# Three changes to the order of work in a one-layer decoder block: the loading of x, the spreading of a block inverse, the place of a router product

## The chip, the core and the metric

The kernel runs on one NeuronCore of a Trainium2 chip. Five engines work side by side, each through its own list of instructions in order: TensorE (PE, matmuls, with a separate column for its weight loads, PEld), VectorE (DVE), ScalarE (ACT), GpSimd (POOL) and SyncE (SP, which here only issues DMAs). ACT and SP both issue DMA transfers; an engine that waits on a semaphore holds up everything behind the wait in its own list. The metric is the device time of one execution in microseconds (us).

## The reference

One layer with 1024 tokens of width 1024, all in fp32. Cut to what matters:

```python
mod = silu(c) @ w_ada + b_ada            # six vectors: shift, scale, gate, twice (adaLN)
h = rmsnorm(x, g1) * (1 + sc1) + sh1
x1 = x + gt1 * hybrid_mixer(h)           # 8 delta-rule heads and a short convolution, gated, then @ w_out
h2 = rmsnorm(x1, g2) * (1 + sc2) + sh2
out = rmsnorm(x1 + gt2 * hierarchical_moe(h2), gf)

# inside hybrid_mixer, for each head and each chunk of 64 tokens
a = where(strict, (k_beta @ k.T) * decay, 0)
t_inv = inverse(eye + a)                 # unit lower triangular
u, w = t_inv @ (v * beta), t_inv @ (k_beta * exp(g))
# then a scan over the chunks with a state of 128x128

# inside hierarchical_moe
g_logits = tok @ w_group + b_group       # 4 groups
e_logits = tok @ w_expert + b_expert     # 32 experts; the best two of the best group
```

## The kernel before

Every engine has its program written out by hand; semaphores order them. A tile of weights is 128 x 8 x 128 values, 512 KB. An fp32 product is made from three matmuls: each weight tile arrives in `w_raw` (a DMA of SP, `load_w`), ACT rounds it into `w_hi` (`split_w_hi`), DVE takes the rest, `w_lo` (`split_w_lo`), and PE multiplies w_lo by hi, w_hi by lo and w_hi by hi (`project`, L662). The token side is split likewise. A raw slot may be loaded again once both its splits are made, and SP issues its loads in order.

**The start.** ACT issues the loads of the eight x tiles of 128 tokens; from the third on it waits for the tile two back. Behind the fourth it waits until PE has transposed the small parameters (`rows_turned`), copies them out (`params`, `conv_w`) and makes `c_act`, the Silu of c. Then follow the other four loads and, tile by tile, Square, Sqrt and, one tile later, the copy of the transposed rows into `x_rows` (`turned_x`, L998). DVE makes the reciprocal and `x_n` (L1377), PE transposes it in two alternating sets of banks. SP meanwhile loads w_ada in sixteen pieces of 512 KB, `ada_sc` and `ada_sh` (`load_shift`, L798), three in flight; DVE multiplies and adds them into one another (`ada_add`, L1356 and L1359), from the fourth x tile on one after each `x_n` and the rest behind the last. When both sums have gone through PE, DVE makes `h_sum`, with which the dense projections begin.

**The heads.** After eight steps of the short convolution and its gate come eight heads, seven of them in a loop and one (`last`) behind it. In a head, the inverses of 16 x 16 diagonal blocks arrive as rows, `inv_rows`; DVE spreads them into block diagonal matrices X and its transpose Y (`spread_inverse`, eight multiplications with a mask each, L1606; the last of X and the last of Y each raise `base_step`). Then three levels (`NL`) double the size of the inverted blocks: PE forms kk_decay times X (L2272), DVE scales it into `LX` (L1678), PE multiplies LX with Y (L2300, L2304), and DVE adds the results to X and Y (L1689, L1692). In the loop's heads PE has a part of a projection behind L2272 in each level; in the last head it has not. Behind the levels stands the scan over the chunks (L2340 on), in which PE also projects other work; in the last head that is `so_hi`, `so_lo`, the last tile of a product that SP reads back from memory (`so_lo<-o_lo_d`, L871). The w_lo splits of two weight tiles of a head stand on either side of `spread_inverse`; in the last head those of the first two tiles of the merge stand behind it.

**The second output projection and the router.** `project_out(n, slot, half)` (L2397) makes half of the mixer's output for token tile n, 24 matmuls; DVE adds it to x (`new_x1`, L1799 and L1804), PE transposes it (`turn_x1`) and multiplies it with the router's weights (`route`). `shift_part` (L2425) multiplies the router's weights, scaled by the shift (`w_shift`, L1788), by ones: sixteen small matmuls, whose sum is an addition to the router's bias. The w_route and b_route that it needs are loaded by SP. The eight token tiles are followed by 32 experts and a final sum, for which SP reads tiles of y with four semaphores, `yg_in`.

Of the kernel before, what the change touches and what calls it, by code (L numbers as in the profile page):

```python
# [12 lines left out]
P = 128  # L13
# [31 lines left out]
def decoder_block(nc, x, c, w_ada, b_ada, norm1_g, w_in, conv_qkv_w, a_log, dt_bias, onorm_g, w_proj_a,  # L45
# [126 lines left out]
    x_t = [at(f"x_t{n}", [P, D]) for n in range(TT // 2)]  # L172
    assert top[0] <= R1
    top[0] = ADA_B
    x_t += [at(f"x_t{n}", [P, D]) for n in range(TT // 2, TT)]
# [203 lines left out]
    with ctx:  # L379
        def sem(name):  # L380
            return ctx.enter_context(nc.semaphore(name))
# [16 lines left out]
        x_in = [sem(f"x_in{s}") for s in range(2)]  # L398
        x_squared = sem("x_squared")
# [126 lines left out]
        yg_in = [sem(f"yg_in{n}") for n in range(4)]  # L526
# [16 lines left out]
                 sc_copied, sc_y_done, gb_sig, root_done, x1T_done, w_mm, *m_out, *h2_out]  # L543

# [236 lines left out]
        def _(sp):  # L781
# [18 lines left out]

            for n in range(KD):
                load_shift(n)
# [169 lines left out]
            for n in range(TT):  # L972
                if n >= 4:
                    sp.wait_ge(yg_in[n % 4], 16)
                sp.dma_start(y_t[:, n].rearrange("p k d -> p (k d)"),
                             y_d[TOP_K * n * P:TOP_K * (n + 1) * P, :].rearrange("(p k) d -> p (k d)", k=TOP_K))\
                    .then_inc(yg_in[n % 4], 16)
# [4 lines left out]
        def _(act):  # L982

            for n in range(TT):
                if n >= 2:
                    act.wait_ge(x_in[n % 2], 16 * (n // 2))
                act.dma_start(x_t[n][:], x_d[n * P:(n + 1) * P, :]).then_inc(x_in[n % 2], 16)
                if n == 3:
                    act.wait_ge(rows_turned, 1)
                    act.activation(params[:], ps[:, 0, 0:97], ACT.Copy).then_inc(cols_ready, 1)  # L990
                    act.activation(conv_w[:].rearrange("p t k h -> p (t k h)"), ps[:, 1, 0:96], ACT.Copy)\
                       .then_inc(cols_ready, 1)
                    act.activation(c_act[:], ps[:, 0, 0:KD], ACT.Silu).then_inc(cols_ready, 1)

            def turned_x(n):
                for a in range(2):
                    act.wait_ge(x_turned, past(2 * n + a + 1))
                    act.activation(x_rows[:, 4 * a:4 * a + 4, n * P:(n + 1) * P],  # L998
                                   ps[:, 2 * (n % 2) + a].rearrange("p (k t) -> p k t", t=P), ACT.Copy)\
                       .then_inc(x_copied, 1)  # L1000

            for n in range(TT):
                act.wait_ge(x_in[n % 2], 16 * (n // 2) + 16)
                if n:
                    act.wait_ge(x_squared, n)
                act.activation(x_sq[:], x_t[n][:], ACT.Square, accum_out=ssq[:, 0, n:n + 1]).then_inc(x_squared, 1)
# [345 lines left out]
        def _(dve):  # L1352
# [16 lines left out]
            for n in range(TT):  # L1369
                col = slice(n, n + 1)  # L1370
                dve.wait_ge(x_root, n + 1)
                dve.reciprocal(ssq[:, 2, col], ssq[:, 1, col]).then_inc(conv_step, 1)

                dve.wait_ge(conv_step, n + 1)
                if n >= 2:
                    dve.wait_ge(x_turned, past(2 * n - 2))
                dve.tensor_scalar(x_n[:, n % 2], x_t[n][:], ssq[:, 2, col], None, ALU.mult).then_inc(x_normed, 1)  # L1377
                if n >= 3:
                    shift_piece(n - 3)
# [272 lines left out]
            def head_dve(h, last):  # L1652
# [12 lines left out]
                if not last:  # L1665
                    split_w_lo(dve, "head", h, 3)
                spread_inverse(h)
                if not last:
                    split_w_lo(dve, "head", h, 4)
                else:  # L1670
                    for p in range(2):
                        split_w_lo(dve, "merge", 0, p)

                for n in range(NL):
                    for a in range(2):
# [5 lines left out]
                        ins.then_inc(lx_done, 1)  # L1681
                    for a in range(2):
# [386 lines left out]
        def _(pe):  # L2069
# [12 lines left out]
            pe.transpose(ps[:, 0, 0:97], rows_a[:], ident[0:97, 0:97])  # L2082
            pe.transpose(ps[:, 1, 0:96], rows_b[:], ident[0:96, 0:96]).then_inc(rows_turned, 1)
# [10 lines left out]
            def turn_x(n):  # L2094
                pe.wait_ge(x_normed, n + 1)
                if n >= 2:
                    pe.wait_ge(x_copied, 2 * (n - 1))
                for k in range(KD):
                    last = pe.transpose(ps[:, 2 * (n % 2) + k // 4, (k % 4) * P:(k % 4 + 1) * P],
# [147 lines left out]
            def head_pe(h, last):  # L2247
# [16 lines left out]
                for n in range(NL):  # L2264
                    for a in range(2):
                        if n == 0:

                            pe.wait_ge(base_step, OPS * h + OPS)
# [20 lines left out]
                    for a in range(2):  # L2289
# [3 lines left out]
                        if n == 0 and a == 0:  # L2293

                            pe.wait_ge(kk_done, 4 * h + 4)
# [270 lines left out]
            for n in range(TT):  # L2566
                pe.wait_ge(w_turned, TOP_K * (n + 1))
                pe.wait_ge(yg_in[n % 4], 16 * (n // 4) + 16)
# [36 lines left out]
```

## Time and profile before

| | |
|---|---|
| median of the runs before | 2142.48 us (3 runs, 2142.0 to 2144.38) |
| the profiled execution | 2141.1 us, its span 2139.3 us |
| PE busy | 2013.1 us, 94% of the span |
| PE weight loads / DVE / ACT / POOL busy | 1683.0 / 1369.7 / 959.1 / 169.6 us |
| moved by DMA | 369.67 MB, mean 173 GB/s |
| mean granted clock of PE | 0.975 of full speed |

The span runs from the first to the last instruction of the profiled execution. PE is busy for nearly all of it, in every one of the page's forty slices but the first and the last few tenths, so what is not PE matters only where PE stands still, where it runs at a lower granted clock, or before its dense work begins. A row of the timeline gives the start, the duration and, in square brackets, the engine's idle time ahead of it and what ended that.

### The profile page before, as it was taken

To read this page: it belongs to the slowest core of one execution; us is meant where nothing else is said; L and a number is where in the kernel's file an instruction comes from. 1 tells how busy PE (TensorE), PEld (TensorE's weight loads), DVE (VectorE), ACT (ScalarE), POOL (GpSimd) and SP (SyncE) were. 2 spreads that over 40 slices of the span, in tenths; PEclk is the share of its full clock that TensorE was granted. 3 is DMA by queue.
4 is the path that set the end of the run, shared out by engine and by line. 5 is a ranking of instruction groups with operands and counts; after the bars stand their busy time and mean duration, and the time that the engine had idled before them with its cause. 6 is when DMAs were issued, how large, how long until landed. Compare 5 with 4: busy or idle time off the path is not lost.

```text
span 2139.3 us, 29380 instructions
## 1 busy us (share of the span) xinstructions
PE 2013.1 (94%) x10107; PEld 1683.0 (79%) x10107; DVE 1369.7 (64%) x2045; ACT 959.1 (45%) x1306; POOL 169.6 (8%) x115
## 2 busy tenths in 40 slices
PE   3799999999999999999999999897899999999995
PEld 2678888888888888888888788786788888888872
DVE  3734453112747558485674735467899999999975
ACT  4221111111443625335253434212588887888863
POOL 0000000000000000000000000000122222222210
PEclk8899999999999999999999999997999999999997
DMA  7224333222202112021120358634899999999955
GB/s 268 69 69 138 99 107 93 76 69 89 55 24 66 51 34 73 23 76 46 39 66 20 96 178 287 194 125 170 287 365 386 378 388 372 387 387 385 399 234 242
DMA packets 209509, 369.67 MB, mean 173 GB/s; under 512 B 43141, under 2 KB 155574, under 8 KB 183862
## 3 DMA queue, kind: packets, MB, share of 16 engines
q1 hardware_dynamic: 190534, 317.63, 42.7%
q10 hardware_dynamic: 9568, 34.63, 4.3%
q0 software_dynamic: 9360, 16.80, 2.1%
q8 instruction: 28, 0.46, 0.1%
q14 instruction: 19, 0.16, 0.0%
HBM read 337.49 MB, written 48.82 MB: 181 GB/s over the span
## 4 chain that ended last, share of the span: by engine, by line
PE 85%; DVE 6%; ACT 4%; issue 2%; DMA 1%; SPq 1%; ACTq 0%; DVEq 0%
PE ps L662 41%; PE ps L2496 16%; PE ps L2534 8%; PE ps L2397 4%; PE ps L2304 2%; PE ps L2272 2%; PE ps L2300 1%; PE ps L2482 1%; DMA x_t<-in_x_dram 1%; ACT w_hi L622 1%; PE ps L2340 1%; PE ps L2311 1%; PE ps L2354 1%; PE ps L2235 1%; PE ps L2255 1%
## 5 line engine op out<-in xcount | busy, mean ns | idle before, releaser
L662 PE MATMUL ps<-h_hi,w_lo 128*128 128x512 f32 x1152 | 463.5, 402 | 3.1 <-DVE h_lo L1414 2.3
L566 DVE TENSOR_TENSOR mw_lo<-mw_raw,mw_hi 128x2048 fp32r<-128x2048 f32 x192 | 436.9, 2290 | 43.2 <-ACT mw_hi L561 43.1
L662 PE MATMUL ps<-h_hi,w_hi 128*128 128x512 f32 x1152 | 449.9, 391 | 0.0
L662 PE MATMUL ps<-h_lo,w_hi 128*128 128x512 f32 x1152 | 449.4, 390 | 0.0
L561 ACT ACTIVATE mw_hi<-mw_raw 128x2048 fp32r<-128x2048 f32 x192 | 368.1, 1919 | 123.1 <-PE ps L2496 73.3
L662 PEld LDWEIGHTS ps<-h_hi,w_hi 128*128 128x128 f32 x1152 | 216.7, 188 | 46.2
L662 PEld LDWEIGHTS ps<-h_hi,w_lo 128*128 128x128 f32 x1152 | 217.3, 189 | 43.4 <-issue 2.4
L662 PEld LDWEIGHTS ps<-h_lo,w_hi 128*128 128x128 f32 x1152 | 217.4, 189 | 39.1
L2496 PE MATMUL ps<-mw_hi,xT_lo 128*128 128x512 f32 x512 | 204.2, 399 | 8.6 <-DVE xT_lo L1977 8.3
L627 DVE TENSOR_TENSOR w_lo<-w_raw,w_hi 128x1024 fp32r<-128x1024 f32 x88 | 107.5, 1223 | 154.0 <-ACT w_hi L622 152.1
L2496 PE MATMUL ps<-mw_hi,xT_hi 128*128 128x512 f32 x512 | 201.2, 393 | 0.0
L2496 PE MATMUL ps<-mw_lo,xT_hi 128*128 128x512 f32 x512 | 200.6, 392 | 0.0
L622 ACT ACTIVATE w_hi<-w_raw 128x1024 fp32r<-128x1024 f32 x88 | 92.1, 1057 | 148.0 <-DVE sc_y L1501 76.2
L2496 PEld LDWEIGHTS ps<-mw_hi,xT_lo 128*128 128x128 f32 x512 | 96.9, 189 | 29.3 <-DVE xT_lo L1977 5.8
L2496 PEld LDWEIGHTS ps<-mw_hi,xT_hi 128*128 128x128 f32 x512 | 96.8, 189 | 21.0
L2496 PEld LDWEIGHTS ps<-mw_lo,xT_hi 128*128 128x128 f32 x512 | 97.0, 190 | 19.4
L751 POOL DMA_INDIRECT xg<-h_d,tok_now x33 | 82.3, 2495 | 315.6 <-DVE tok_now L1967 297.6
L2534 PE MATMUL ps<-mw_hi,hidT_lo 128*128 128x512 f32 x256 | 103.2, 403 | 2.1 <-DVE hidT_lo L1991 2.1
L2534 PE MATMUL ps<-mw_lo,hidT_hi 128*128 128x512 f32 x256 | 100.3, 392 | 0.0
L2534 PE MATMUL ps<-mw_hi,hidT_hi 128*128 128x512 f32 x256 | 100.2, 391 | 0.0
L1089 ACT ACTIVATE gate_a<-ps 128x512 f32<-128x512 f32 x16 | 9.6, 597 | 159.1 <-PE ps L662 159.1
L1540 DVE SCALAR_TENSOR_TENSOR qk<-conv_in,hconv,qk 128x512 f32<-128x512 f32 x96 | 73.6, 767 | 2.9
(373 smaller groups left out, 3208.3 us busy)
## 6 DMA issues: line engine op xcount, KB each, us to landing
mw_raw<-in_w_dram SPq DMA_DIRECT2D x192, 1024.0 KB, 7.8
w_raw<-in_w_in_dram SPq DMA_DIRECT2D x72, 512.0 KB, 4.1
ada_b<-in_w_ada_dram SPq DMA_DIRECT2D x8, 2048.0 KB, 8.0
y_t<-y_d SPq DMA_DIRECT2D x8, 1024.0 KB, 10.0
x_t<-in_x_dram ACTq DMA_DIRECT2D x8, 512.0 KB, 6.5
ada_sc<-in_w_ada_dram SPq DMA_DIRECT2D x8, 512.0 KB, 6.4
ada_sh<-in_w_ada_dram SPq DMA_DIRECT2D x8, 512.0 KB, 6.0
w_raw<-in_w_proj_b_dram SPq DMA_DIRECT2D x8, 512.0 KB, 3.7
```

Of the source, the lines that this page charges most:

```text
L561: act.activation(mw_hi[off % NSPLIT][:], mw_raw[off % NRAW][:], ACT.Copy).then_inc(mw_hi_done, 1)
L566: dve.tensor_tensor(mw_lo[off % NSPLIT][:], mw_raw[off % NRAW][:], mw_hi[off % NSPLIT][:], ALU.subtract).then_inc(mw_lo_done, 1)
L622: act.activation(w_hi[:, t["slot"]], w_raw[:, t["slot"]], ACT.Copy).then_inc(w_hi_done, 1)
L627: dve.tensor_tensor(w_lo[:, t["slot"]], w_raw[:, t["slot"]], w_hi[:, t["slot"]], ALU.subtract).then_inc(w_lo_done, 1)
L662: last = pe.matmul(dst, lhs[:, s, k], rhs[:, k, cols], start=(k == 0 and part == 0), stop=(k == KD - 1 and part == 2))
L751: pool.indirect_dma_start(xg[:, s], None, h2_d, bass.IndirectOffsetOnAxis(tok_now[:, s:s + 1], axis=0), bounds_check=T - 1, oob_is_err=Fal ...
L1540: dve.scalar_tensor_tensor(out=dst[:, lo:hi], in0=src, scalar=w, in1=dst[:, lo:hi], op0=ALU.mult, op1=ALU.add).then_inc(steps, 1)
L2272: last_mm = pe.matmul(ps[:, 6 + a, (t % 4) * P:(t % 4 + 1) * P], kk_decay[:, t], X[:, t], start=True, stop=True)
L2304: last_mm = pe.matmul(half_dst(2 + a, t, n), LX[:, t], blocks_of(Y[:, t], n, 1), start=True, stop=True)
L2397: last = pe.matmul(ps[:, 2 * s + half], lhs, rhs[:, k, half * HALF:(half + 1) * HALF], start=(k == 0 and part == 0), stop=(k == KD - 1 and ...
L2496: last = pe.matmul(dst, lhs[:, k0 + k], rhs[:, cols], start=(first and k == 0 and part == 0), stop=(final and k == 3 and part == 2))
L2534: last = pe.matmul(ps[:, 5 + half], lhs[:, 2 * part + f], rhs[:, cols], start=(part == 0 and f == 0 and n == 0), stop=(part == 1 and f == ...
```

## The change

The order of work is changed in three places; what is computed stays.

**At the start** ACT issues all of x without a wait: two tiles of 512 KB and then three pairs of 1 MB, each pair with a semaphore of its own (`tile_in`, which also serves the final sum in place of `yg_in`). SP waits for the first pair before the first piece of w_ada. The parameters are transposed into banks 6 and 7, and `c_act` is made ahead of the two copies. PE's transposes of x use three sets of banks, and the copy of a tile's rows follows two tiles later.

**In the heads** `spread_inverse` comes directly behind q_dec; the two splits follow the scaling of LX in levels 0 and 1. PE waits for X alone ahead of L2272 and for Y ahead of its first use.

**At the router** `shift_part` moves from ahead of `project_out(1, 1, 0)` to behind it.

```diff
+            sp.wait_ge(tile_in[0], 16)
             for n in range(KD):
                 load_shift(n)
...
-            for n in range(TT):
-                if n >= 2:
-                    act.wait_ge(x_in[n % 2], 16 * (n // 2))
-                act.dma_start(x_t[n][:], x_d[n * P:(n + 1) * P, :]).then_inc(x_in[n % 2], 16)
-                if n == 3:
-                    act.wait_ge(rows_turned, 1)
-                    act.activation(params[:], ps[:, 0, 0:97], ACT.Copy).then_inc(cols_ready, 1)
-                    act.activation(conv_w[:].rearrange("p t k h -> p (t k h)"), ps[:, 1, 0:96], ACT.Copy)\
-                       .then_inc(cols_ready, 1)
-                    act.activation(c_act[:], ps[:, 0, 0:KD], ACT.Silu).then_inc(cols_ready, 1)
+            for n in range(2):
+                act.dma_start(x_t[n], x_d[n * P:(n + 1) * P, :]).then_inc(x_in[n], 16)
+            for n in range(1, TT // 2):
+                act.dma_start(x_pairs[n][:], x_d[2 * n * P:2 * (n + 1) * P, :].rearrange("(a p) d -> p a d", p=P))\
+                   .then_inc(tile_in[n - 1], 16)
+            act.wait_ge(rows_turned, 1)
+            act.activation(c_act[:], ps[:, 6, 0:KD], ACT.Silu).then_inc(cols_ready, 1)
+            act.activation(params[:], ps[:, 6, 0:97], ACT.Copy).then_inc(cols_ready, 1)
+            act.activation(conv_w[:].rearrange("p t k h -> p (t k h)"), ps[:, 7, 0:96], ACT.Copy).then_inc(cols_ready, 1)
...
-                if n:
-                    turned_x(n - 1)
-            turned_x(TT - 1)
+                if n >= 2:
+                    turned_x(n - 2)
+            for n in range(TT - 2, TT):
+                turned_x(n)
...
-                if not last:
-                    split_w_lo(dve, "head", h, 3)
                 spread_inverse(h)
-                if not last:
-                    split_w_lo(dve, "head", h, 4)
-                else:
-                    for p in range(2):
-                        split_w_lo(dve, "merge", 0, p)
...
                         ins.then_inc(lx_done, 1)
+                    if n < 2:
+                        split_w_lo(dve, *(("merge", 0, n) if last else ("head", h, 3 + n)))
...
-                if n >= 2:
-                    pe.wait_ge(x_copied, 2 * (n - 1))
+                if n >= 3:
+                    pe.wait_ge(x_copied, 2 * (n - 2))
...
-                            pe.wait_ge(base_step, OPS * h + OPS)
+                            pe.wait_ge(base_step, OPS * h + OPS - 1)
...
                         if n == 0 and a == 0:
 
+                            pe.wait_ge(base_step, OPS * h + OPS)
                             pe.wait_ge(kk_done, 4 * h + 4)
...
-            pe.wait_ge(rows_in, 16 * 7)
-            pe.wait_ge(m_step, past(3 * KD))
-            shift_part()
             for n in range(1, TT):
                 project_out(n, n % 2, 0)
+                if n == 1:
+                    pe.wait_ge(rows_in, 16 * 7)
+                    pe.wait_ge(m_step, past(3 * KD))
+                    shift_part()
                 turn_x1(n - 1)
                 project_out(n, n % 2, 1)
```

ACT's list from its first instruction, before (the number behind a name tells buffers apart; a square bracket holds the semaphores that are waited for):

```order
L987 DMA x_t_95<-in_x_dram 128x1024
L987 DMA x_t_96<-in_x_dram 128x1024
L987 DMA x_t_97<-in_x_dram 128x1024 [waits x_in0]
L987 DMA x_t_98<-in_x_dram 128x1024 [waits x_in1]
L990 ACT_TABLE_LOAD
L990 ACTIVATE params<-ps 128x97 [waits rows_turned]
L991 ACTIVATE conv_w<-ps 128x96
L993 ACT_TABLE_LOAD
L993 ACTIVATE c_act<-ps 128x8
L987 DMA x_t_99<-in_x_dram 128x1024 [waits x_in0]
```

and now:

```order
L991 DMA x_pair_95<-in_x_dram 128x1024 x2
L993 DMA x_pair_96<-in_x_dram 128x2x1024
L993 DMA x_pair_97<-in_x_dram 128x2x1024
L993 DMA x_pair_98<-in_x_dram 128x2x1024
L996 ACT_TABLE_LOAD
L996 ACTIVATE c_act<-ps 128x8 [waits rows_turned]
L997 ACTIVATE params<-ps 128x97
L998 ACTIVATE conv_w<-ps 128x96
L1014 ACTIVATE x_sq,ssq<-x_pair_95 128x1024 [waits x_in0]
```

The loads have lost their waits, one table load and both copies stand behind the Silu's, and the first Square follows at once.

DVE's list in the first head of the loop, behind the product q_dec, before (register instructions left out):

```order
L1663 TENSOR_TENSOR q_dec<-qk,grow 128x1024 [waits silu_done]
L627 TENSOR_TENSOR w_lo<-w_raw,w_hi 128x1024 [waits w_hi_done]
L1606 TENSOR_TENSOR X<-inv_rows,sub_mask 128x128 [waits base_moved]
L1606 TENSOR_TENSOR X<-inv_rows,sub_mask 128x128 x7
L1606 TENSOR_TENSOR Y<-inv_rows,sub_mask 128x128 [waits base_step]
L1606 TENSOR_TENSOR Y<-inv_rows,sub_mask 128x128 x7
L627 TENSOR_TENSOR w_lo<-w_raw,w_hi 128x1024 [waits w_hi_done]
L1678 SCALAR_TENSOR_TENSOR LX<-ps,hk,level_mask 128x128 [waits lx_mm]
L1678 SCALAR_TENSOR_TENSOR LX<-ps,hk,level_mask 128x128 x3
```

and now:

```order
L1672 TENSOR_TENSOR q_dec<-qk,grow 128x1024 [waits silu_done]
L1615 TENSOR_TENSOR X<-inv_rows,sub_mask 128x128 [waits base_moved]
L1615 TENSOR_TENSOR X<-inv_rows,sub_mask 128x128 x7
L1615 TENSOR_TENSOR Y<-inv_rows,sub_mask 128x128 [waits base_step]
L1615 TENSOR_TENSOR Y<-inv_rows,sub_mask 128x128 x7
L1680 SCALAR_TENSOR_TENSOR LX<-ps,hk,level_mask 128x128 [waits lx_mm]
L1680 SCALAR_TENSOR_TENSOR LX<-ps,hk,level_mask 128x128 x3
L1680 SCALAR_TENSOR_TENSOR LX<-ps,hk,level_mask 128x128 [waits lx_mm]
L1680 SCALAR_TENSOR_TENSOR LX<-ps,hk,level_mask 128x128 x3
L632 TENSOR_TENSOR w_lo<-w_raw,w_hi 128x1024 [waits w_hi_done]
L1693 TENSOR_TENSOR X<-X,ps 128x16x16 [waits yl_mm,xl_mm]
```

Both splits have left the stretch between q_dec and LX; the first one stands between LX and the update of X in level 0, the second likewise in level 1.

PE's list between the end of `project_out(0, 0, 1)` and what follows, before:

```order
L2397 MATMUL ps<-wo_lo,m_hi 128x512
L2397 MATMUL ps<-wo_hi,m_hi 128x512
L2425 MATMUL ps<-w_shift,ones 128x36 [waits r_step,m_step,rows_in]
L2425 MATMUL ps<-w_shift,ones 128x36 x7
L2397 MATMUL ps<-wo_hi,mt_lo_171 128x512 [waits x1_done,mt_in1]
L2397 MATMUL ps<-wo_lo,mt_hi_170 128x512
```

and now, from the end of `project_out(1, 1, 0)`:

```order
L2402 MATMUL ps<-wo_lo,m_hi 128x512
L2402 MATMUL ps<-wo_hi,m_hi 128x512
L2430 MATMUL ps<-w_shift,ones 128x36 [waits r_step,m_step,rows_in]
L2430 MATMUL ps<-w_shift,ones 128x36 x7
L2411 MATMUL ps<-ident,x_151 128x128 [waits x1T_done,x1_done]
L2411 MATMUL ps<-ident,x_151 128x128 x7
L2402 MATMUL ps<-wo_hi,mt_lo_167 128x512
```

The sixteen matmuls of `shift_part` now have the transposes of `turn_x1(0)` directly behind them, and 24 matmuls of the projection more ahead.

## Rows read from the trace of the kernel before

**Rows 1.** The page's part 4: the chain that ended last, by engine.

```profile
PE 85%; DVE 6%; ACT 4%; issue 2%; DMA 1%; SPq 1%; ACTq 0%; DVEq 0%
```

**Rows 2.** Timeline, 0 to 85 us: start, duration, engine, line, out<-in, [idle before <-releaser].

```profile
4.30 16.62 SPq L798 DMA_DIRECT2D ada_sc<-in_w_ada_dram  x8
10.48 0.39 PE L2082 MATMUL ps<-ident,rows_a 97*128 97x97 f32 x1 [10.48 <-DMA dt_row<-in_dt_bias_dram]
11.48 1.28 ACT L993 ACT_TABLE_LOAD   x1
21.62 1.06 ACT L1006 ACTIVATE x_sq<-x_t 128x1024 f32<-128x1024 f32 x1 [8.67 <-DMA x_t<-in_x_dram]
23.14 16.34 SPq L798 DMA_DIRECT2D ada_sh<-in_w_ada_dram  x8
36.77 1.06 ACT L998 ACTIVATE x_rows<-ps 128x512 f32<-128x512 f32 x2
42.04 0.75 DVE L1377 TENSOR_SCALAR x_n<-x_t,ssq 128x1024 f32<-128x1024 f32 x1
68.45 0.77 PE L662 MATMUL ps<-h_hi,w_lo 128*128 128x512 f32 x1 [2.33 <-DVE h_lo L1414]
```

**Rows 3.** Waits of ACT, 0 to 40 us: total, times, longest.

```profile
ACT x_rows L998 <- PE ps L2099: 1.6, 4, 1.0
```

**Rows 4.** Windows: PE, PEld, DVE, ACT, POOL busy (x), PEclk, DMA share, GB/s.

```profile
8.00:24.00 16.00, 0.55 (x2) 0.29 (x2) 0.00 (x0) 4.21 (x7) 0.00 (x0) 1.00 1.01 407
```

**Rows 5.** The tile ada_sh: its eight transfers.

```profile
DMA to landing us min/median/max: 4.1/6.0/9.6
```

**Rows 6.** Timeline of head 1 of the loop, DVE and PE.

```profile
668.41 1.22 DVE L1663 TENSOR_TENSOR q_dec<-qk,grow 128x1024 f32<-128x1024 f32 x1
670.24 1.22 DVE L627 TENSOR_TENSOR w_lo<-w_raw,w_hi 128x1024 fp32r<-128x1024 f32 x1 [0.61 <-ACT w_hi L622]
671.38 1.70 DVE L1606 TENSOR_TENSOR X<-inv_rows,sub_mask 128x128 f32<-128x128 f32 x8
674.88 2.05 PE L2272 MATMUL ps<-X,kk_decay 128*128 128x128 f32 x16 [1.76 <-DVE Y L1606]
680.15 0.42 DVE L1689 TENSOR_TENSOR X<-X,ps 128x256 f32<-128x256 f32 x1 [1.91 <-PE ps L2304]
687.59 0.42 DVE L1689 TENSOR_TENSOR X<-X,ps 128x256 f32<-128x256 f32 x1 [2.62 <-PE ps L2304]
```

**Rows 7.** Waits, 100 to 1470 us: total, times, longest.

```profile
PE ps L2272 <- DVE Y L1606: 12.3, 7, 1.8
```

**Rows 8.** Timeline of the last head: SP, DVE and PE.

```profile
1223.48 0.56 SPq L871 DMA_DIRECT2D so_lo<-o_lo_d  x1
1224.71 2.36 DVE L627 TENSOR_TENSOR w_lo<-w_raw,w_hi 128x1024 fp32r<-128x1024 f32 x2 [7.54 <-ACT w_hi L622]
1228.16 1.10 PE L2300 MATMUL ps<-LX,Y 128*128 128x64 f32 x8 [3.35 <-DVE LX L1678]
1247.26 0.46 PE L2340 MATMUL ps<-v_beta,Y 128*128 128x128 f32 x2
```

**Rows 9.** The tile so_lo in the last head: its transfer.

```profile
DMA to landing us min/median/max: 21.6/21.6/21.6
```

**Rows 10.** Windows in and behind the last head, columns as in rows 4.

```profile
1228.00:1236.00 8.00, 7.84 (x41) 7.84 (x42) 2.65 (x9) 0.00 (x0) 0.00 (x0) 0.58 1.02 415
1264.00:1272.00 8.00, 5.05 (x22) 3.38 (x21) 1.34 (x2) 5.09 (x8) 0.00 (x0) 1.00 0.62 192
```

**Rows 11.** Timeline of the router's beginning, PE and DVE.

```profile
1367.62 3.60 PE L2425 MATMUL ps<-w_shift,ones 128*128 128x36 f32 x16 [4.95 <-DVE w_shift L1788]
1369.37 1.28 DVE L1804 TENSOR_TENSOR x<-x,xr 128x512 f32<-128x512 f32 x2
```

**Rows 12.** The chain in order of time behind them: project_out(1, 1, 0) and the next half.

```profile
1371.23 7.87 PE ps L2397 x24
1379.97 5.46 PE ps L2397 x24
```

More of the change, by code:

```diff
@@ L171, in decoder_block @@
     ssq = at("ssq", [P, 3, TT])
-    x_t = [at(f"x_t{n}", [P, D]) for n in range(TT // 2)]
+    x_pairs = [at(f"x_pair{n}", [P, 2, D]) for n in range(2)]
     assert top[0] <= R1
     top[0] = ADA_B
-    x_t += [at(f"x_t{n}", [P, D]) for n in range(TT // 2, TT)]
+    x_pairs += [at(f"x_pair{n}", [P, 2, D]) for n in range(2, 4)]
+    x_t = [x_pairs[n // 2][:, n % 2] for n in range(TT)]
     top[0] = SCRATCH
@@ L398, in decoder_block @@
         x_in = [sem(f"x_in{s}") for s in range(2)]
+        tile_in = [sem(f"tile_in{n}") for n in range(4)]
         x_squared = sem("x_squared")
@@ L524, in decoder_block @@
         y_out = [sem(f"y_out{n}") for n in range(2)]
-        yg_in = [sem(f"yg_in{n}") for n in range(4)]
         w_turned = sem("w_turned")
@@ L543, in decoder_block, with tile_arrivals @@
                  sc_copied, sc_y_done, gb_sig, root_done, x1T_done, w_mm, *m_out, *h2_out]
+        def tile_arrivals(n):
+            return 16 * (n // 4) + (32 if n % 4 < TT // 2 - 1 else 16)
         def past(n):
@@ L998, in turned_x @@
                     act.activation(x_rows[:, 4 * a:4 * a + 4, n * P:(n + 1) * P],
-                                   ps[:, 2 * (n % 2) + a].rearrange("p (k t) -> p k t", t=P), ACT.Copy)\
+                                   ps[:, 2 * (n % 3) + a].rearrange("p (k t) -> p k t", t=P), ACT.Copy)\
                        .then_inc(x_copied, 1)
             for n in range(TT):
-                act.wait_ge(x_in[n % 2], 16 * (n // 2) + 16)
+                if n < 2:
+                    act.wait_ge(x_in[n], 16)
+                else:
+                    act.wait_ge(tile_in[n // 2 - 1], 16)
                 if n:
                     act.wait_ge(x_squared, n)
-                act.activation(x_sq[:], x_t[n][:], ACT.Square, accum_out=ssq[:, 0, n:n + 1]).then_inc(x_squared, 1)
+                act.activation(x_sq[:], x_t[n], ACT.Square, accum_out=ssq[:, 0, n:n + 1]).then_inc(x_squared, 1)
                 act.wait_ge(x_squared, n + 1)
@@ L1376, in _ @@
                     dve.wait_ge(x_turned, past(2 * n - 2))
-                dve.tensor_scalar(x_n[:, n % 2], x_t[n][:], ssq[:, 2, col], None, ALU.mult).then_inc(x_normed, 1)
+                dve.tensor_scalar(x_n[:, n % 2], x_t[n], ssq[:, 2, col], None, ALU.mult).then_inc(x_normed, 1)
                 if n >= 3:
@@ L2081, in _ @@
             pe.wait_ge(params_in, 16 * 9)
[L2082 to L2083 removed]
+            pe.transpose(ps[:, 6, 0:97], rows_a[:], ident[0:97, 0:97])
+            pe.transpose(ps[:, 7, 0:96], rows_b[:], ident[0:96, 0:96]).then_inc(rows_turned, 1)
             pe.wait_ge(cols_ready, 3)
@@ L2095, in turn_x @@
                 pe.wait_ge(x_normed, n + 1)
-                if n >= 2:
-                    pe.wait_ge(x_copied, 2 * (n - 1))
+                if n >= 3:
+                    pe.wait_ge(x_copied, 2 * (n - 2))
                 for k in range(KD):
-                    last = pe.transpose(ps[:, 2 * (n % 2) + k // 4, (k % 4) * P:(k % 4 + 1) * P],
+                    last = pe.transpose(ps[:, 2 * (n % 3) + k // 4, (k % 4) * P:(k % 4 + 1) * P],
                                         x_n[:, n % 2, k * P:(k + 1) * P], ident[:])
```

7 lines of the change are left out of this document (4 added, 3 removed).

## The prediction

> **What bounds the kernel now.** I began with the chain of work that ended last: 85% of it is PE (TensorE) [rows 1]. Time is won only where PE waits or crawls, or where nothing on PE has started yet, so I read the timeline at the three places that the change touches and asked at each what came last.
>
> The start: the first rmsnorm Square sits on ACT at 21.62, behind 8.67 us of waiting for x, and the dense stream of matmuls begins at 68.45 [rows 2]. Between them DVE (VectorE) is the chain: its last x_n is at 42.04 and its list of adaLN pieces runs on from there [rows 2]. The DMA engines are full from 8 to 24 us, at 407 GB/s [rows 4], yet ACT has only issued its loads one by one. The heads: in seven of eight, PE waits 1.8 us for DVE's Y, 12.3 us in all [rows 7]. The router: PE idles 4.95 us for w_shift and then works slowly for a while [rows 11, 12].
>
> The sum is made against the profiled execution, 2141.1 us with a span of 2139.3; the median of the runs is 2142.48, so 1.4 is added at the end.
>
> **Part A, the start.** The x loads now stand in ACT's queue one behind the other, and the only wait before Square 0 is that of c_act for the parameter transposes. Before, these PE transposes began at 10.48, the moment the last small parameter transfer landed, and the table load for the Silu stood behind the two copies, at 11.48 for 1.28 us [rows 2]. Now the table load comes ahead of the wait; three small activations end at about 11.6, and Square 0 can start there, if tile 0 is in. x is 4.19 MB, 10.3 us at 407 GB/s [rows 4]; from about 2.0 it is whole by 12.3, or by 13.5 with the parameters and a slow start between, and tile 0 is in long before. Gain 21.62 − 11.6 = 10.0. Two smaller ones follow: the copies of a tile's rows stand a tile later in ACT's list, so ACT's waits for PE's transposes, 1.6 us in four [rows 3], go; and ahead of the last x_n one pair of copies fewer stands on ACT, 2 × 0.53 = 1.06, of which I count 0.95 [rows 2]. A: 10.0 + 1.6 + 0.95 = about **12.7**, and DVE's list behind x_n(7) moves with it unchanged.
>
> What could take it back is the adaLN stream: SP now waits for the first pair of x, landing at about 8.4 by the same rate, where its first ada load was issued at 4.30 [rows 2]. So it starts 4.1 later. Before, the last ada_sh was issued at 23.14 + 16.34 = 39.5 and landed 6.0 (at most 9.6) later [rows 2, 5], while sharing the engines with x. Now x is out of the way at 12.3 and the sixteen pieces and two weight tiles, 9.4 MB, need 23 us at 407 GB/s: in by about 36 to 40. Their last use, 61.2 before, comes at 48.5: covered by at least 8 us. If the cover were gone, each us of lateness would cost one.
>
> Ends of A: parameters landing only once x is whole, at 13.5, put Square 0 at 13.5 + 1.1 = 14.6, so A is 7.0 + 2.6 = 9.6. Parameters landing with the first x tile, at about 7.2, put it at 8.3, so A is 13.3 + 2.6 = 15.9. I take 10.48, since that landing was seen while x tiles and ada pieces were in flight.
>
> A rule of the Trainium skill speaks against this. By "DMA: Bandwidth & Descriptors", section "Queues, rings and completion order", a transfer's semaphore count is written only after every earlier write of that DMA engine, across its queues. Parameters could then not be reported before the x data queued ahead on each engine, which is the 9.6 end. No row here decides that.
>
> **Part B, seven heads.** In head 1 q_dec ends at 669.63; DVE then waited for w_hi, split w_lo from 670.24, and did X at 671.38 for 1.70 and Y [rows 6]. With the split gone from there X ends at 671.3 and Y at 673.1, and PE, which was free at 674.88 − 1.76 = 673.12, waits only for X. The whole wait goes: 7 × 1.76 = **12.3** [rows 6, 7]. The splits (2.36 / 2 = 1.18 each [rows 8]) now lie after the LX scaling of levels 0 and 1, where DVE idled 1.91 and 2.62 [rows 6]: 0.7 and 1.4 of cover are left; were the first gone, PE would wait for X and Y by the excess only. SP's reloads of those raw slots move 6 to 8 us later; their next reader is ACT's w_hi of the following head, whose own product q_dec is a whole head away. Ends: 10.5 to 12.3.
>
> **Part B, the last head.** Here two splits waited for late w_hi until 1224.71 and kept PE until 1228.16, 3.35 idle; then PE crept at a mean clock of 0.58 for 8 us, losing 8 × 0.42 = 3.4 [rows 8, 10]. Both go, 6.5 us with the short wait for LX that stays: PE would reach the scan, 1247.26 before, at about 1240.8. But the scan first needs so_lo from memory: issued at 1223.48, landing 21.6 later, at 1245.1 [rows 8, 9]. Nothing ahead of that issue moves, relative to the head. So the scan starts at 1245.2: gain 2.1, with a new PE wait of about 4.3. Waits of 3.35 and 4.95 were each followed by half clock [rows 8, 10, 11, 12], while in 1264 to 1272, where PE was busy only 5.05 of 8 us, the clock stayed at 1.00 [rows 10]. 4.3 is above the first, so I expect the dense scan at half clock at first: 3.4 lost there, 1.8 + 2.4 at the router (below), mean 3.7. Net 2.1 − 3.7 = **−1.6**. Ends: −2.5 and +2.1.
>
> The Trainium skill, "TensorE: Matmul & The Clock Gate", section "HAM oscillation — how this bites in real kernels", says that waits for a DMA between bursts of matmuls throttle the engine again and again. By it I get the same −1.6; no half clock gives +2.1, the second rival.
>
> **Part C, the router.** PE was free at 1367.62 − 4.95 = 1362.67 and waited for w_shift, whose operand landed late. Then shift_part took 3.60 for 16 matmuls and the 24 matmuls behind it 7.87, where 24 take 5.46 at full clock [rows 11, 12]. Now project_out(1, ·, 0) fills 1362.67 to 1368.1; w_shift is ready at 1367.5, so shift_part follows without a wait at full clock, 1.8, to 1369.95. turn_x1(0) then waits for x1 tile 0, which ends at 1369.37 + 1.28 = 1370.65 [rows 11]: idle 0.7. Before, turn_x1(0) began after 1371.23 + 7.87 = 1379.0 (a last matmul's tail aside) [rows 12]. Gain 1379.0 − 1370.7 = **8.3**; I count 8.2. Behind it PE sets the pace. Ends: if the clock still falls over these 24 matmuls, 8.3 − 2.4 = 5.9; if x1 comes earlier, up to 9.0.
>
> Sum: 12.7 + 12.3 − 1.6 + 8.2 = **31.6**. 2141.1 − 31.6 = 2109.5, with the 1.4 2110.9.
>
> **The rivals.** (1) Parameters are reported only after x: for it, x's writes are now all queued ahead; against it, they landed in the midst of full DMA engines before. A is 9.6: 2110.9 + 3.1 = 2114.0. (2) The last head's wait brings no half clock: for it, the window at 1264; against it, the 3.35. 2110.9 − 3.7 = 2107.2. (3) Parameters land early, since no ada traffic competes until 8.4: A is 15.9, 2110.9 − 3.2 = 2107.7; before they landed at 10.48 with light traffic from 4 to 8, which speaks for something slow in the small transfers themselves. (4) Slower: in each head the w_lo split blocks DVE in the level loop, because its w_hi comes late, and PE waits there. Its point is a PE wait of 3.35, from which half clock follows: 3.35 + 3.4 = 6.75 in seven heads, 47, less the 31.6 gained leaves +15.7, 2158. For it, DVE did wait for w_hi(h,3) by 0.61 [rows 6]; against it, w_hi was there at 670.24 and is now asked for at 675. (5) The change doesn't do what it says at the start, because the ada stream and not x sets the end of DVE's list: with the last piece in at 56 and not by 40, 7.7 later than its use at 48.5, A would be 5.0, the time 2118.6. Against it, the 8 us of cover.
>
> **How the numbers follow.** Forecast 0.52; (1) 0.17; (2) 0.13; (3) 0.08; (5) 0.07; (4) and anything else slower 0.02; 0.01 for no difference. A measurement of this kernel can tell some 0.2%, 4.3 us, from no change; all but the last 0.03 lie far under 2138. The range reaches from (2) and (3) together, 2104.0, to (1) with the lower end of C, 2116.4, and a little beyond: 2103 to 2119, which also takes in (5).
>
> **What would show it.** In the profile after: Square 0 at 11 to 12.5 and not at 14; x_n(7) near 29.5; the dense stream near 55.8; ada pieces never the releaser of DVE. No row of PE's LX product waiting for Y in the heads, none for X. One wait of 4 us at the last head's scan, released by so_lo's transfer, with the clock down behind it. At the router no wait of 4.95, shift_part at 1.8, turn_x1(0) waiting under 1 us for x1. Wrong it would be if PE rows in the level loop are released by DVE's X or Y updates, or if the stage between 40 and 56 us stretches.

## The result and the profile after

The changed kernel takes 2110.87 us in the median (4 runs, 2109.61 to 2113.15), beside 2143.09 (4 runs) for the kernel before on the same chip: a ratio of 0.9853, with a 95% interval of 0.9841 to 0.9865, or 32.2 us less. The forecast was 2110.9. Its sum is right, but three of its four terms are not: the start gave a third less than forecast, the seven heads more, and the last head came out near nothing where a loss of 1.6 was forecast. That the errors cancelled is luck.

The profiled execution is the slowest of the four (span 2111.2), and that of the kernel before, 2141.1 us, lay under the lowest of the four runs beside it (2142.0), so the rows below add up to 28.1 and not to 32.2. Read it in the same order. First the page's part 4, the chain that ended last (compare [rows 1]): PE has grown from 85% to 87% and DMA from 1% to 4%; so_lo and pieces of w_ada are among the transfers on it. For the w_ada pieces this is no wait: no DVE row of the start is released by one.

```profile
PE 87%; DVE 4%; DMA 4%; ACT 3%; issue 1%; ACTq 0%; SPq 0%; DVEq 0%; POOLq 0%
```

The start, from the timeline of after (compare [rows 2]):

```profile
1.69 1.67 ACTq L993 DMA_DIRECT2D x_pair<-in_x_dram  x3
3.38 1.28 ACT L996 ACT_TABLE_LOAD   x1 [3.38 <-issue]
10.04 14.47 SPq L803 DMA_DIRECT2D ada_sc<-in_w_ada_dram  x8
14.92 0.40 PE L2086 MATMUL ps<-ident,rows_a 97*128 97x97 f32 x1 [14.92 <-DMA dt_row<-in_dt_bias_dram]
15.84 1.07 ACT L1014 ACTIVATE x_sq<-x_pair 128x1024 f32<-128x1024 f32 x1
33.32 0.75 DVE L1386 TENSOR_SCALAR x_n<-x_pair,ssq 128x1024 f32<-128x1024 f32 x1
59.74 0.76 PE L667 MATMUL ps<-h_hi,w_lo 128*128 128x512 f32 x1 [2.33 <-DVE h_lo L1423]
```

ACT has issued all of x by 3.4 us and then stands still: the parameters, forecast for 10.5, are there at 14.92, so Square 0 comes at 15.84 instead of 11.6. The two smaller gains behind it come as forecast: Square 0 is 5.8 earlier than before, the last x_n 8.7, and the first dense matmul 8.7. When x itself landed is in the tile's own view (two single tiles and three pairs, from issue to landing):

```profile
DMA to landing us min/median/max: 3.3/8.3/15.5
```

The longest, 15.5, is the third pair, issued at 2.65: x is whole only at 18.2, and not at 12.3 to 13.5. Its first pair was in at 10.0, for 8.4 forecast, and from then on w_ada pieces are loaded beside the rest. The second pair, issued at 2.15, took 11.9 and was in at 14.1. So the parameters were reported 0.9 behind the second pair and 3.2 ahead of the third.

The heads, head 1 of the loop on DVE and PE (compare [rows 6]):

```profile
658.13 1.22 DVE L1672 TENSOR_TENSOR q_dec<-qk,grow 128x1024 f32<-128x1024 f32 x1
659.27 1.70 DVE L1615 TENSOR_TENSOR X<-inv_rows,sub_mask 128x128 f32<-128x128 f32 x8
662.45 0.40 PE L667 MATMUL ps<-h_hi,w_hi 128*128 128x512 f32 x1
662.68 1.95 PE L2276 MATMUL ps<-X,kk_decay 128*128 128x128 f32 x16
665.85 1.22 DVE L632 TENSOR_TENSOR w_lo<-w_raw,w_hi 128x1024 fp32r<-128x1024 f32 x1
667.85 0.42 DVE L1693 TENSOR_TENSOR X<-X,ps 128x256 f32<-128x256 f32 x1 [0.78 <-PE ps L2309]
```

PE no longer waits at the LX product, and DVE, with the split done, still waits 0.78 for PE: the cover held. The product starts at 574.00 in the first head and at 1106.11 in the seventh, six periods of 88.68 us; before it was 584.13 and 1128.62, six of 90.75. The last head and the router, on PE and SP (compare [rows 8, 11]):

```profile
1200.85 0.56 SPq L877 DMA_DIRECT2D so_lo<-o_lo_d  x1
1222.63 0.76 PE L2345 MATMUL ps<-v_beta,Y 128*128 128x128 f32 x2 [4.03 <-DMA so_lo<-o_lo_d]
1348.65 1.87 PE L2430 MATMUL ps<-w_shift,ones 128*128 128x36 f32 x16
1350.36 1.09 PE L2411 MATMUL ps<-ident,x 128*128 128x128 f32 x8
```

The scan starts 24.63 earlier than before (2.0 more than the head's first product with X, 1222.87 before and 1200.23 now), behind the wait of 4 us for so_lo that was forecast. The transposes of x1 tile 0, 1378.93 before, start 28.6 earlier. Two windows, with the columns of [rows 4], show PE at half clock for a part of each:

```profile
1222.00:1230.00 8.00, 7.37 (x29) 6.52 (x30) 0.64 (x2) 1.11 (x4) 0.00 (x0) 0.59 0.55 137
1246.00:1254.00 8.00, 7.24 (x16) 4.48 (x17) 0.97 (x2) 4.38 (x5) 0.00 (x0) 0.60 0.50 173
```

The first is the scan behind the wait for so_lo, as forecast. The second was not: it follows a wait of 2.8 for the sums of squares, which the kernel before has too, at full clock [rows 10].

### The profile page after: what moved, and what is told of

Its sections match the earlier page's. It is cut to its first block, busy times and chain, and to the rows that moved or that the text cites. A ratio compares the mean times of both kernels' runs of the same rounds, so it can differ in the third digit from the quotient of the medians.

```text
span 2111.2 us, 29382 instructions
## 1 busy us (share of the span) xinstructions
PE 2007.2 (95%) x10107; PEld 1679.6 (80%) x10107; DVE 1367.3 (65%) x2045; ACT 957.4 (45%) x1305; POOL 169.4 (8%) x115
## 4 chain that ended last, share of the span: by engine, by line
PE 87%; DVE 4%; DMA 4%; ACT 3%; issue 1%; ACTq 0%; SPq 0%; DVEq 0%; POOLq 0%
PE ps L667 43%; PE ps L2502 17%; PE ps L2540 8%; PE ps L2402 4%; PE ps L2276 2%; PE ps L2309 2%; PE ps L2488 1%; PE ps L2305 1%; DMA so_lo<-o_lo_d 1%; DMA ada_sh<-in_w_ada_dram 1%; PE ps L2345 1%; DMA ada_sc<-in_w_ada_dram 1%; PE ps L2359 1%; PE ps L2239 1%; PE ps L2259 1%
## 5 line engine op out<-in xcount | busy, mean ns | idle before, releaser
L1707 DVE SCALAR_TENSOR_TENSOR S<-S,hgate,ps 128x128 f32<-128x128 f32 x48 | 16.7, 348 | 92.7 <-PE ps L2357 92.7
```

## The experiments

In diffs "-" is the changed kernel and "+" the experiment, unless it is said otherwise. The kernel before ran beside each group, at a median of 2143.5 to 2143.9. The medians of the kernel before, the first group's 2143.09 with them, lie within 0.8, so a kernel of one group may be held against the changed kernel's 2110.87 of another. Differences of less than 2 us between two medians of four runs are not read as anything, since the runs of one kernel spread over 1.7 to 9 us.

**Each part undone.** The start undone (shown are the loads; the banks, the order of the copies and of c_act are put back with them):

```diff
-            sp.wait_ge(tile_in[0], 16)
...
-            for n in range(2):
-                act.dma_start(x_t[n], ...).then_inc(x_in[n], 16)
-            for n in range(1, TT // 2):
-                act.dma_start(x_pairs[n][:], ...).then_inc(tile_in[n - 1], 16)
+            for n in range(TT):
+                if n >= 2:
+                    act.wait_ge(x_in[n % 2], 16 * (n // 2))
+                act.dma_start(x_t[n][:], ...).then_inc(x_in[n % 2], 16)
```

> The changed kernel with part A (the start) put back as it was before; heads and router stay changed. What is undone here is what part A is worth. The forecast's A is 12.7, so the time would be 2110.9 + 12.7 = 2123.6, and the parameter transposes on PE are back at about 10.5. The trace of the changed kernel has its first dense matmul at 59.74 where it was at 68.45, which makes A 8.7 and the time 2119.6. If the parameters' late landing there (14.92) was a matter of that one execution and not of the order of transfers, the median behind it would hold more than that trace shows, and the time is nearer to 2123.6.

It took 2119.29 (4 runs), 8.4 more than the changed kernel. The transposes of the parameters are early again, and the dense work late:

```profile
9.63 0.39 PE L2077 MATMUL ps<-ident,rows_a 97*128 97x97 f32 x1 [9.63 <-DMA dt_row<-in_dt_bias_dram]
68.30 0.76 PE L662 MATMUL ps<-h_hi,w_lo 128*128 128x512 f32 x1 [2.33 <-DVE h_lo L1414]
```

So A is worth 8.4 to 8.7 and not 12.7, and the parameters' late landing is no chance: every trace with the new loading has the transposes between 13.71 and 14.92 (six traces, where no wait is added), every one with the old between 9.48 and 10.48 (four). In all six the parameters were reported between two pairs of x: 0.3 to 1.1 behind the landing of the second and 3.2 to 3.8 ahead of that of the third.

The router's part undone:

```diff
+            pe.wait_ge(rows_in, 16 * 7)
+            pe.wait_ge(m_step, past(3 * KD))
+            shift_part()
             for n in range(1, TT):
                 project_out(n, n % 2, 0)
-                if n == 1:
-                    pe.wait_ge(rows_in, 16 * 7)
-                    pe.wait_ge(m_step, past(3 * KD))
-                    shift_part()
```

> The changed kernel with shift_part back ahead of project_out(1, 1, 0). Forecast of C 8.2, the two traces 8.3 (turn_x1(0) 28.65 earlier, w_shift 20.35 earlier): 2110.9 + 8.2 = 2119.1, with a wait of PE for w_shift near 5 and the 24 matmuls behind at about 7.9. If the clock alone and not the wait made the gain (the 24 matmuls now elsewhere at half clock), 2115. Its start is that of the changed kernel: the parameter transposes on PE at about 14.9 if the order of the transfers decides, near 10.5 if that was one execution's chance.

2116.06, 5.2 more than the changed kernel, with so wide a spread (2111.84 to 2120.87) that the forecast 8.2 is not excluded. In its profiled execution, the fastest of the four, PE came to the router later, relative to w_shift, than in the kernel before:

```profile
1328.58 0.77 PE L2402 MATMUL ps<-wo_hi,mt_lo 128*128 128x512 f32 x1 [2.31 <-DMA mt_lo<-m_lo_d]
1342.59 1.95 PE L2430 MATMUL ps<-w_shift,ones 128*128 128x36 f32 x16 [1.39 <-DVE w_shift L1792]
```

A wait of 2.31 for mt_lo was followed by half clock (0.77 for a matmul instead of 0.39). From that matmul to the wait for w_shift PE took 12.6 us, for 11.2 in the kernel before; and from the landing of mt_lo to w_shift's end it was 2.1 less than there (14.01 for 16.10). So only 1.39 of the wait for w_shift was left, and shift_part ran at full clock. w_shift itself waits for b_route, a transfer, so what PE loses ahead of it is not lost twice.

The heads' part undone, in all eight heads:

```diff
+                if not last:
+                    split_w_lo(dve, "head", h, 3)
                 spread_inverse(h)
+                if not last:
+                    split_w_lo(dve, "head", h, 4)
+                else:
+                    for p in range(2):
+                        split_w_lo(dve, "merge", 0, p)
...
-                    if n < 2:
-                        split_w_lo(dve, *(("merge", 0, n) if last else ("head", h, 3 + n)))
...
-                            pe.wait_ge(base_step, OPS * h + OPS - 1)
+                            pe.wait_ge(base_step, OPS * h + OPS)
...
-                            pe.wait_ge(base_step, OPS * h + OPS)
```

> The changed kernel with part B undone in all eight heads. By the forecast B is 12.3 - 1.6 = 10.7: 2121.6. By the traces the head period fell from 90.75 to 88.68, 2.07 in each of seven heads and thus 14.5, and between the last head's first LX product and the router 2.3 were lost (22.64 gained before it, 20.35 behind): 12.2, or 2123.1. If the half clock at the last head's scan costs nothing that counts, 2125. The wait of PE for Y is back at 1.76 in seven heads, the last head's at 3.35, and no wait for so_lo.

2125.95, 15.1 more, beyond the forecast's 10.7. PE's waits, of its trace (total, times, longest):

```profile
PE ps L2281 <- DVE Y L1615: 12.3, 7, 1.8
PE ps L2309 <- DVE LX L1687: 3.6, 2, 3.3
```

And the last head's part alone:

```diff
                 spread_inverse(h)
+                if last:
+                    for p in range(2):
+                        split_w_lo(dve, "merge", 0, p)
...
-                    if n < 2:
-                        split_w_lo(dve, *(("merge", 0, n) if last else ("head", h, 3 + n)))
+                    if n < 2 and not last:
+                        split_w_lo(dve, "head", h, 3 + n)
```

> The changed kernel with the two w_lo splits of the last head back between Y and LX; the seven heads of the loop stay changed. The forecast holds that part of the change for a loss of 1.6 (2.1 gained, 3.7 lost to half clock), so undoing it gives 2109.3; by the traces it loses 2.3, so 2108.6. The rival of no half clock would make it slower by 2.1, 2113.0. In its trace PE waits 3.35 ahead of the first L x Y product with half clock behind it, reaches the scan within 0.5 of so_lo's landing or later, and runs the scan at full clock; the 2.8 wait of the sums of squares behind the scan is followed by full clock as in the kernel before, if the half clock there in the changed kernel hangs on what stood ahead of it.

2110.70 (2109.62 to 2115.01), no difference (0.2). This part of the change gives nothing that the medians can tell; by themselves they exclude neither the forecast loss of 1.6, which is under the 2 us, nor clearly the rival's gain of 2.1, and the traces have to say more. Its trace has half clock in the level loop and none in the scan, the changed kernel the other way round:

```profile
1204.65 1.97 PE L2308 MATMUL ps<-LX,Y 128*128 128x64 f32 x8 [3.35 <-DVE LX L1683]
1224.73 0.46 PE L2348 MATMUL ps<-v_beta,Y 128*128 128x128 f32 x2
```

**One part alone.** The kernel before with the router's part:

> The kernel before with part C alone. By the forecast it is worth 8.2: 2143.3 - 8.2 = 2135.1. Taken back from the changed kernel it cost 5.2 by the medians (2116.06 against 2110.87), and in that kernel's trace PE came late to the router by its half clock at the last head's scan and behind the merge, so that only 1.4 of the wait for w_shift was left. If the two hide one another, C alone is worth its 8.2 here, where the scan runs at full clock; if C is worth 5 in any case, the time is 2138. In its trace no wait for w_shift, shift_part at 1.9, and a wait of under 1 for x ahead of turn_x1(0).

2135.30 beside 2143.91, a gain of 8.6 (ratio 0.9962, 0.9948 to 0.9976). So C alone is worth its 8.2; the median of 5.2 with it undone may be smaller because PE's lateness hides a part of the wait, as in the trace above, or by the spread. The kernel before with the heads' part:

> The kernel before with part B alone. The forecast's B is 10.7: 2143.3 - 10.7 = 2132.6. Taken back from the changed kernel it cost 15.1 by the medians. From starts of matmuls the head period fell by 2.05 in seven heads, 14.4; the last head's part was about 0 (0.2 by the medians of its own run); at the router the half clock at the last scan lets PE come late and shortens the wait for w_shift, so that B alone may show up to 2 more here than 14.4: 2143.3 - 14.4 to 16.4 = 2126.9 to 2128.9. In its trace the wait for w_shift is under 4.95.

2129.01 beside 2143.75, a gain of 14.7 (0.9937, 0.9920 to 0.9955). Its trace had a wait of 4.65 for w_shift, so PE's lateness at the router in the trace of the run with the router's part undone was that of its execution and not a fixed consequence of the heads' part. The sum 8.4 + 14.7 + 8.6 = 31.7 is near the 32.2 of the whole. With all three undone singly it is 8.4 + 15.1 + 5.2 = 28.7.

**What holds the parameters back.** One wait on ACT ahead of the three pairs of x:

```diff
+            act.wait_ge(params_in, 16 * 9)
             for n in range(1, TT // 2):
                 act.dma_start(x_pairs[n][:], ...)
```

> The changed kernel with one wait added on ACT: behind the first two x tiles it waits for the nine parameter transfers before it issues the three pairs. In the four traces with the new loading the parameter transposes began at 13.71 to 14.92, in the two with the old one at 9.63 and 10.48. If the x data queued ahead holds the small transfers back, they now land early, the transposes stand at 6 to 8 and Square 0 at 7 to 9; the pairs come later, the last x_n near 28 to 30 instead of 33.32, and the time is 3 to 5 under the changed kernel, 2106 to 2108. The cover of the ada pieces gets thin: SP's wait for the first pair moves their start to about 12, and their last one may become DVE's releaser near 48, which would keep 1 to 2 of that. If the small transfers are slow by themselves, the transposes stay at 10 or later, the pairs are issued there, and the time is the changed kernel's, 2110 to 2112.

2107.57, 3.3 less than the changed kernel. The small transfers land at 7.29 now, with 1 MB of x ahead of them instead of 4 (timeline, and waits of DVE from 0 to 62 us):

```profile
7.29 0.39 PE L2087 MATMUL ps<-ident,rows_a 97*128 97x97 f32 x1 [7.29 <-DMA dt_row<-in_dt_bias_dram]
27.75 0.75 DVE L1387 TENSOR_SCALAR x_n<-x_pair,ssq 128x1024 f32<-128x1024 f32 x1
55.46 0.77 PE L667 MATMUL ps<-h_hi,w_lo 128*128 128x512 f32 x1 [2.33 <-DVE h_lo L1424]
...
DVE ada_sh L1369 <- DMA ada_sh<-in_w_ada_dram: 1.6, 2, 1.1
DVE ada_sh L1366 <- DMA ada_sh<-in_w_ada_dram: 1.6, 1, 1.6
```

The last x_n is 5.6 earlier than in the changed kernel, the dense work 4.3: DVE now waits for ada pieces, so their cover is used up here. In the changed kernel it was about 5 us: the first piece of ada_sh landed at 34.6 and was used at 39.35, the last at 47.1 and 52.49. Here their uses come 5.6 earlier and their loads begin at 12.09 instead of 10.04. With this wait the start gains 68.45 − 55.46 = 13.0 on the kernel before. So x queued ahead holds the parameters back. How it does so, by sharing the engines or by counts that wait for some of its writes, is not told apart; that they wait until x is whole is out, by the landings above.

```diff
-            sp.wait_ge(tile_in[0], 16)
+            sp.wait_ge(params_in, 16 * 9)
...
+            act.wait_ge(params_in, 16 * 9)
```

> As the run before it, with SP's first ada load waiting for the parameter transfers in place of the first pair of x. The ada stream then starts at 6 to 8 and shares the engines with the pairs. If the ada pieces were what the last run ended on, this is faster than it by 1 to 2; if not, the pairs land later by the 1.5 MB of ada in flight beside them, some 3 to 4, the x_n of tiles 2 to 7 wait for them, and it is slower than the last run by up to 3.

2107.58, the same. The ada pieces, issued from 7.13 on, hold DVE no more, but ACT waits 1.1 for pairs of x; the dense work starts at 55.56.

**What the wait for so_lo costs.** The same bytes in two parts, with a semaphore that is free by then:

```diff
-            for dst, src in ((so_hi, o_hi_d), (so_lo, o_lo_d)):
-                sp.dma_start(dst[:, 0:H - 1]..., src...[:, 0:H - 1]).then_inc(o_in, 16)
+            for lo_k, hi_k, arrived in ((0, 3, o_in), (3, H - 1, x_in[0])):
+                for dst, src in ((so_hi, o_hi_d), (so_lo, o_lo_d)):
+                    sp.dma_start(dst[:, lo_k:hi_k]..., src...[:, lo_k:hi_k]).then_inc(arrived, 16)
...
                     if last:
+                        if n == 3:
+                            pe.wait_ge(x_in[0], 48)
```

> The changed kernel with the read back of so_hi and so_lo in two parts each: rows of three heads first, of four behind them, and PE waits for the first part ahead of the last head's scan and for the second at its fourth piece of filler. The bytes are the same. PE's wait of 4.0 to 4.4 for so_lo ahead of the scan goes, since the first part, 3.1 MB, lands near 10 instead of 21.5 after its issue. If that wait is what brought half clock to the scan (0.59 to 0.69 in the four traces that have it, 1.00 in the three that have not), the scan runs at 1.00 and the time is lower by 4.0 + 3 = 7, up to 10 in executions where half clock came back after the wait of 2.8: 2101 to 2104. If half clock comes without the wait, it is lower by 4: 2107. If the second part lands late, PE waits inside the scan instead, and little is gained.

2104.53, 6.3 less than the changed kernel. The scan starts 18.25 behind the head's first product with X (1200.44 to 1218.69) instead of 22.40, and runs at full clock:

```profile
1218.69 0.46 PE L2348 MATMUL ps<-v_beta,Y 128*128 128x128 f32 x2
1217.00:1225.00 8.00, 7.97 (x53) 6.97 (x53) 1.06 (x3) 2.48 (x8) 0.00 (x0) 1.00 1.09 349
...
DMA to landing us min/median/max: 10.4/15.6/20.8
```

The first part lands 10.4 after its issue, the second 20.8 after its own, and neither is waited for. Of the 6.3, 4.1 is the wait, and 2.2 to 2.3 what half clock costs in the scan: from the scan's first matmul to turn_x1(0) it is 123.21 here and 123.23 with the last head's part undone, both at full clock, and 125.54 in the second trace of the changed kernel (below). The scan by itself, from its first product of v_beta and Y to its last, took 17.51, 17.21 and 19.49, which makes 2.0 to 2.3.

**The changed kernel again, and both additions.**

> The changed kernel as it is, beside the next two on the same chip, and a second trace of it. If the parts add up (8.4, 15.1, and 8.6 for the router alone, 32.1), it stands at 2111 again, and its parameter transposes between 13.7 and 14.9. The half clock behind the wait of 2.8 that followed the last scan in its first trace (0.60) is there again if it belongs to the kernel, and not if it falls by chance from one execution to the next, as it was in one of two traces with the same work there.

2109.70 (2108.73 to 2114.09) beside 2143.75, 34.1 less; a span of 2107.1 in the profiled execution, 4.1 less than the first one's. The parameters' transposes are at 14.43, and the wait for so_lo, 4.00, has half clock behind it again. The wait of 2.8 behind the scan has not, this time:

```profile
1220.00:1228.00 8.00, 6.55 (x27) 5.83 (x28) 0.56 (x2) 0.88 (x4) 0.00 (x0) 0.59 0.67 170
1244.00:1252.00 8.00, 6.79 (x26) 5.00 (x27) 2.73 (x3) 4.83 (x5) 0.00 (x0) 1.00 0.50 183
```

> The changed kernel with both additions: ACT waits for the parameters ahead of the three pairs of x (3.3 by its own run) and so_hi, so_lo are read back in two parts (6.3 by its own run). They lie at two ends of the program, so they add: 2110.9 - 9.6 = 2101.3. In the trace the transposes at 7.3, the first dense matmul near 55.5, no wait at the scan, and full clock there.

2102.48 (2100.93 to 2102.64), ratio to before 0.9805 (0.9788 to 0.9821): 8.4 less than the changed kernel's first median and 7.2 less than the one beside it, of 9.6 expected. In its trace the transposes are at 7.50, the first dense matmul at 55.20, no wait stands before the scan, and the clock there is full; but half clock follows the wait of 2.8 behind it.

> As the run before it, with SP's first ada load waiting for the parameters in place of the first pair of x. The two forms of the start gave 2107.57 and 2107.58, so 2101.3 here too; no wait of DVE for ada pieces, which took 3.2 in the other form's trace, and three short waits of ACT for x instead.

2103.14 (2099.76 to 2104.68), ratio 0.9813: the same, and as expected without a wait of DVE for ada pieces. Both forms beat the kernel before and the changed kernel; four runs of each don't tell which of the two is better.

## Why the prediction was right, point by point

**The start: the order of work right, the landing wrong, 4.3 too large.** The step that failed is "I take 10.48, since that landing was seen while x tiles and ada pieces were in flight". It took a landing seen with four tiles of x issued, the last two of them singly behind landings, for one with all eight queued; it was 13.7 to 14.9. The two steps behind it, 2.6 us, measured 2.9 (8.72 at the last x_n less 5.78 at Square 0). The three terms of the forecast, 10.0, 1.6 and 0.95, moreover add up to 12.55 and not to 12.7.

The time was near that of rival (1), 9.6 forecast and 8.4 to 8.7 measured, to which I had given 0.17, but its event did not happen: the parameters were not reported "only after x". Their last transfer was issued at 3.85, behind all three pairs, and was reported 3.2 to 3.8 ahead of the third pair's landing in the six traces. The conclusion that the prediction drew from the Trainium skill, "Parameters could then not be reported before the x data queued ahead on each engine", pointed to the right end of the range and went too far: the rule speaks of earlier writes, and the third pair was queued ahead but not yet written. That the rival's number came near is luck: x, expected whole at 13.5, was whole at 17.5 to 18.5. The gain that the forecast took for granted was then had by one wait more (13.0 by traces). Of the ada pieces the event is right, DVE waited for none; the cover was about 5 us and not 8, since the last piece landed at 47.1 and not by 40.

**The seven heads: right, 2.2 too small.** The wait went whole, and more than its row came back. The row [rows 7] gives 1.76 a head; the head's period fell by 2.07. Before, the last matmul ahead of the wait started at 672.73 and the LX product at 674.88, 2.15 later; after, 662.45 and 662.68, 0.23 later. That is 1.92, and from the product's start to the next matmul's it was 1.80 and is now 1.70: 2.02. The idle time of a row begins where the modelled end of a matmul lies, 0.39 behind its start, while the next would have started after 0.23. The weight loads' own wait for Y in the kernel before says it more nearly, in a view that was read and not used:

```profile
PEld ps L2272 <- DVE Y L1606: 15.3, 7, 2.2
```

Seven times 2.07 is 14.5, and the runs with and without part B, the last head in them, say 14.7 and 15.1.

**The last head: the events right, the price not.** A wait of 4.0 for so_lo, released by its transfer, and half clock behind it came as forecast, in all of the seven traces that have this wait. The gain up to the scan was 2.0 by rows of before and 3.0 by the run with this part undone (25.37 from the head's first product with X to the scan there, 22.36 in the second trace of the changed kernel), for 2.1; half clock in the level loop had lasted 9.0 us there and 6.8 in the kernel before. The term that failed is the price of half clock, 3.7. It was taken from stretches of 6.8 and 8.4 us at half clock, and in the scan the clock was full again after 2.9 to 5.9 us. From the scan's first product of v_beta and Y to its last it took 18.51 to 19.86 in the seven traces with the wait and 17.21 to 17.51 in the seven without, so 1.0 to 2.6 were lost, as in these rows of the last product, 19.86 behind the first in the changed kernel and 17.51 with so_lo in two parts:

```profile
1242.49 0.38 PE L2345 MATMUL ps<-v_beta,Y 128*128 128x128 f32 x2
1236.20 0.38 PE L2348 MATMUL ps<-v_beta,Y 128*128 128x128 f32 x2
```

The net is near 0 and not −1.6. Why the clock came back sooner here is open. Rival (2), no half clock, is out.

**The router: right.** 8.2 in the traces (turn_x1(0) 28.57 earlier, w_shift 20.35), 8.6 by the kernel with this part alone, for 8.2. That it may shrink when taken out of the changed kernel, to 5.2 by a wide spread, was not foreseen.

**What was not in the forecast at all** is the spread. In the first trace of the changed kernel half clock followed the wait of 2.8 behind the scan, in the second not; from the last head's first product with X to turn_x1(0) they took 150.1 and 147.9. All fourteen traces have this wait, and half clock followed it in four.

Rival (3), parameters early, is out with their landing at 13.7 to 14.9. The slower rival (4) has nothing for it: with the seven heads changed no PE row between 62 and 1450 us is released by DVE's X or Y in any trace. Nor has (5): no DVE row of the changed kernel waits for an ada piece.

## What to carry to other kernels

In this kernel a transfer that is small and early in its own queue was not early while another queue held megabytes: issue what the first consumer needs, wait for it, and only then queue the bulk. Cost a stall of TensorE by the starts of the matmuls on either side or by its weight loads, not by the idle time of its row alone, and price half clock by how long it lasts where it falls. And a sum that comes out right says nothing of its terms: undo each part, and do it alone as well, since two parts may wait for the same DMA.

## What the runs showed of the hardware

- The same nine small transfers, 0.1 MB in all, issued by SP from 0.79 to 4.3 us, landed at 7.25 to 7.5 with two tiles of x (1 MB) issued ahead of them by ACT, at 9.5 to 10.5 with four tiles of x issued by 5.8 and ada pieces behind the parameters, and at 13.7 to 14.9 with all 4.19 MB of x issued by 3.4, which itself was whole at 17.5 to 18.5.
- PE's clock fell to half after each wait of 4.0 to 4.95 (nine) and of 3.35 (four), for 2.9 to 9.0 us. After one and the same wait of 2.8 it fell in four traces of fourteen, and once after one of 2.31. So the granted clock behind the same wait can differ from one execution to the next, and one profile of such a kernel is not its median: the spans of two executions of the changed kernel differ by 4.1 us, of which 2.2 lie there.
